# The same tiles at other addresses: small SBUF tiles first, a filler, and every large tile at a multiple of 2048 bytes

## The reference

```python
x = first_block(...)   # modulated rmsnorm, w_in, causal pooling + chunked state-space mixer, w_out, then PEER
x = second_block(...)  # rmsnorm, w_in (7 x 1024 columns), RG-LRU + gated conv, w_out, then PEER, rmsnorm
def peer(h, ...):      # product-key retrieval of single-neuron experts, 8 heads, top 16 of 16384 experts
    s1, s2 = q1 @ sub_keys1.T, q2 @ sub_keys2.T      # 128 + 128 keys per head
    idx, gates = top16 of (top16(s1) + top16(s2)), softmax
    act = gelu(h . expert_down[idx]);  out = sum(gates * act * expert_up[idx])
```

## Time and profile before

| | |
|---|---|
| median of 3 runs | 2038.16 us (2026.67, 2038.16, 2045.39) |
| profiled execution, its own time | 2028.78 us |
| its span, first to last instruction | 2027.0 us |
| TensorE matmul busy | 1974.7 us, 97% of the span |
| VectorE / ScalarE busy | 1506.5 us (74%) / 1013.7 us (50%) |
| granted TensorE clock, mean | 0.99 |
| DMA | 440.82 MB, mean 217 GB/s |

### The profile page before, as it was taken

One profiled execution on the slowest core, in us unless ns is written; L12 is line 12 of the kernel. 1 busy time (PEld: TensorE's weight loads), 2 busy tenths in 40 slices (PEclk: granted clock), 3 DMA queues, 4 the chain that ended last, 5 costly groups with the idle time before them and its releaser, 6 DMA issues.

```text
span 2027.0 us, 37752 instructions
## 1 busy us (share of the span) xinstructions
PE 1974.7 (97%) x14131; PEld 1830.3 (90%) x14131; DVE 1506.5 (74%) x2593; ACT 1013.7 (50%) x1358; POOL 0.2 (0%) x4
## 2 busy tenths in 40 slices
PE   7999899999999999999999999999999999999998
PEld 6988899999999888888799999999999998888886
DVE  5766769987886666666679665699878866666666
ACT  3651444455555444454546554444555554444444
POOL 0000000000000000000000000000000000000000
PEclk8999999999999999999999999999999999999999
DMA  7645767776556778777655654788766567777776
GB/s 269 207 169 206 270 194 249 243 240 213 182 182 212 244 238 243 240 241 244 209 167 155 189 158 145 229 248 240 242 209 183 181 214 242 240 242 240 237 246 197
DMA packets 135020, 440.82 MB, mean 217 GB/s; under 512 B 14976, under 2 KB 15232, under 8 KB 131200
## 3 DMA queue, kind: packets, MB, share of 16 engines
q1 hardware_dynamic: 117056, 406.84, 64.4%
q10 hardware_dynamic: 17856, 32.51, 4.4%
HBM read 403.64 MB, written 35.65 MB: 217 GB/s over the span
## 4 chain that ended last, share of the span: by engine, by line
PE 89%; DVE 6%; DMA 3%; ACT 2%; issue 1%; SPq 0%; DVEq 0%; ACTq 0%
PE ps L553 27%; PE ps L554 27%; PE ps L555 27%; PE ps L847 3%; DVE ring_lo L371 2%; DMA ring<-in_w_in 2%; PE ps L590 1%; ACT ring_hi L365 1%; PE ps L696 1%; DVE arena L1840 1%; PE ps L823 1%; PE ps L546 0%; DMA ring<-in_down 0%; DVE arena L1351 0%; DMA xT<-kept_x_spill 0%
## 5 line engine op out<-in xcount | busy, mean ns | idle before, releaser
L371 DVE TENSOR_TENSOR ring_lo<-ring,ring_hi 128x1024 fp32r<-128x1024 f32 x632 | 772.4, 1223 | 298.4 <-ACT ring_hi L365 290.4
L365 ACT ACTIVATE ring_hi<-ring 128x1024 fp32r<-128x1024 f32 x632 | 668.1, 1057 | 623.5 <-PE ps L555 470.3
L553 PE MATMUL ps<-h_hi,ring_lo 128*128 128x256 f32 x2816 | 799.0, 284 | 20.4 <-DVE ring_lo L371 9.4
L554 PE MATMUL ps<-h_lo,ring_hi 128*128 128x256 f32 x2816 | 786.8, 279 | 0.0
L555 PE MATMUL ps<-h_hi,ring_hi 128*128 128x256 f32 x2816 | 786.7, 279 | 0.0
L553 PEld LDWEIGHTS ps<-h_hi,ring_lo 128*128 128x128 f32 x2816 | 535.5, 190 | 24.9 <-issue 20.8
L554 PEld LDWEIGHTS ps<-h_lo,ring_hi 128*128 128x128 f32 x2816 | 535.2, 190 | 0.4 <-issue 0.2
L555 PEld LDWEIGHTS ps<-h_hi,ring_hi 128*128 128x128 f32 x2816 | 532.7, 189 | 0.0
L555 PE MATMUL ps<-ring_hi,w_hi 128*128 128x512 f32 x1024 | 398.4, 389 | 0.0
L554 PE MATMUL ps<-ring_lo,w_hi 128*128 128x512 f32 x1024 | 398.4, 389 | 0.0
L553 PE MATMUL ps<-ring_hi,w_lo 128*128 128x512 f32 x1024 | 398.4, 389 | 0.0
(11 more groups left out here) (284 smaller groups left out, 1287.7 us busy)
## 6 DMA issues: line engine op xcount, KB each, us to landing
ring<-in_down SPq DMA_DIRECT2D x256, 512.0 KB, 4.3
ring<-in_up SPq DMA_DIRECT2D x256, 512.0 KB, 4.0
ring<-in_w_in SPq DMA_DIRECT2D x80, 512.0 KB, 3.7
kept_z<-wf ACTq DMA_DIRECT2D x124, 256.0 KB, 3.3
xT<-kept_z SPq DMA_DIRECT2D x124, 256.0 KB, 4.3
arena<-in_w_ada SPq DMA_DIRECT2D x24, 1024.0 KB, 10.1
ring<-in_wq SPq DMA_DIRECT2D x32, 512.0 KB, 4.3
ring<-in_w_out_ssd SPq DMA_DIRECT2D x8, 512.0 KB, 4.2
```

The costliest lines, as they stand in the source:

```text
L365: nc.scalar.activation(ring_hi[:, part_slot(m), :], ring[:, slot(m), :], ACT.Copy).then_inc(S("high"), 1)
L371: ns.tensor_tensor(ring_lo[:, part_slot(n), :], ring[:, slot(n), :], ring_hi[:, part_slot(n), :].bitcast(fp32), ALU.subtract)\
L553: mm(psum, s_lo, m_hi, start=start, stop=False)
L554: mm(psum, s_hi, m_lo, start=False, stop=False)
```

## The change

The thirteen small tiles (`prm`, `iota16`, `ident16`, `mask16`, `mod`, `cact`, `epsc`, `lru_s`, `gain`, `sums_of`, `eps2`, `roots`, and a new one of 400 bytes that nobody reads or writes, `gap`) are allocated before all others. They end at byte 4096 of each partition with the 1152 bytes taken before and the rounding. All other tiles follow in the order they had. No instruction is added, removed or moved on any engine, and none has another shape: only the addresses in them differ.

```diff
+        prm = sb("prm", [P, NCOL])
+        iota16 = sb("iota16", [P, HD, 2], fp16)
+        ident16 = sb("ident16", [P, P], bf16)
+        mask16 = sb("mask16", [P, P], bf16)
+        mod = sb("mod", [P, 48])
+        cact = sb("cact", [P, 8])
+        epsc = sb("epsc", [P, 1])
+        lru_s = sb("lru_s", [P, 8, 8])
+        gain = sb("gain", [P, KC])
+        sums_of = sb("sums_of", [P, KC, 2])
+        eps2 = sb("eps2", [P, 2])
+        roots = sb("roots", [P, TT, 2])
+        gap = sb("gap", [P, 100])
         xT = sb("xT", [P, KC, T])
 
         h_hi = sb("h_hi", [P, KC, T], fp32r)
         h_lo = sb("h_lo", [P, KC, T], fp32r)
-        prm = sb("prm", [P, NCOL])
         cst = sb("cst", [P, NCONST])
         ring = sb("ring", [P, RING, BLK])
...
         sel16 = sb("sel16", [P, T // 4, 2, 2, 4, 2], fp16)
-        iota16 = sb("iota16", [P, HD, 2], fp16)
...
-        lru_s = sb("lru_s", [P, 8, 8])
         xs_lo = sb("xs_lo", [P, KC, T], fp32r)
-        gain = sb("gain", [P, KC])
...
-        roots = sb("roots", [P, TT, 2])
```

More of the change, by code:

```diff
@@ L104, in decoder_kernel @@
         sel16 = sb("sel16", [P, T // 4, 2, 2, 4, 2], fp16)
-        iota16 = sb("iota16", [P, HD, 2], fp16)
[L106 to L110, removed]
-        lru_s = sb("lru_s", [P, 8, 8])
         xs_lo = sb("xs_lo", [P, KC, T], fp32r)
-        gain = sb("gain", [P, KC])
-        sums_of = sb("sums_of", [P, KC, 2])
-        eps2 = sb("eps2", [P, 2])
-        roots = sb("roots", [P, TT, 2])
         ps_all = ctx.enter_context(nc.psum_tensor("ps", [P, 8, 512], fp32))
```

## The result

The change made the kernel slower: 2061.9 us (median of 4 runs, 2061.05 to 2063.38) against 2034.76 us (4 runs, 2026.67 to 2045.39), a ratio of 1.0134 with a 95% interval of 1.0098 to 1.017. The profiled execution took 2061.34 us with a span of 2059.5 us, 32.5 us more than before. The forecast was 25 us less; what came was most of the rival in which the two streams of TensorE collide.

A forecast was written before the change was run, and what follows sets the result against it. PE, busy 97% of the span, was taken to bound the kernel through the pace of the split products. 2028.8 - 20.6 - 3.9 = 2004.3 us, with 4.7 added for the median, gave 2009 us; range 1978 to 2068 us.

The forecast's parts named there:

- What bounds the kernel: PE is busy 97% of the span; only a changed pace of the split products can move the time by much.
- Up products: 3072 multiplies of 512 columns, moving tile from rest 64 to 0: 6.7 ns less each, 20.6 us; bounds 0 and 41.
- Residual products: 576 multiplies with `w_hi`, `w_lo` or `xs_lo` moving go from 120.0 to 113.3 ns: 3.9 us less.
- The `h_hi`/`h_lo` products: 8448 multiplies, moving tile already at rest 0 by 128: taken as 0; bounds 13 us less, 43 us more.
- The slower rival: Moving reads collide with next weights' loading at equal rests; `h_hi` products go to 120.0 ns, 43 us more, 2076 us; chance 0.22.
- No change: Rival: the paces 120.0 and 226.7 come from something other than the address; about 2034 us; chance 0.34.
- Faster still: Rival: up products reach 213.3 ns and the slow pace of `h_hi` products ends; 1971 us; chance 0.10.
- All other work: VectorE and ScalarE durations differ below 1% by address, 2 us at most; DMA taken as 0.
- The spread: The runs' spread of 19 us fits the two paces of the `h_hi` products and was expected to stay.

The follow-up runs named there:

- those at 64 and 192: The changed kernel with `h_hi` and `h_lo` moved to a rest of 64 or of 192 bytes: 2044.87 us (ratio 1.0064) and 2031.44 us (ratio 0.9988).
- the last kernel: The changed kernel with `w_hi` and `w_lo` moved by 64 bytes, so the up products get a difference of 192: 2081.01 us, ratio 1.0257.
- the one at 112: The changed kernel with `h_hi` and `h_lo` at a rest of 112 by 256, other large tiles at 0: 2019.75 us, ratio 0.9947.
- the mixed pairs: Stand-alone streams with tiles of one pair at different offsets: `m_lo` alone at 64 took 120.1 ns, `m_hi` 118.9, `s_hi` 122.1, `s_lo` 117.8.

## Why the prediction was wrong

**What bounds the kernel** was right: only the pace of the split products could move the time, and it did.

**The step that failed is "Up products", and "Residual products" with it.** The 120.0 ns of `w_hi`/`xs_lo` against the 113.3 ns of `h_hi` was read as the rest of the *moving* tile by 128. It was a difference of 0 against one of 192 to the *stationary* tile. The prediction said itself that the rows couldn't part the two. Forecast were -20.6 and -3.9 us; the up products moved by 0.0 us (696.16 both times, 884 records both times), the residual products by nothing that counts (120.0 ns still, their sum 1.9 us longer). Their difference was 0 before and after. The bounds of the first, 0 and -41 us, held by their upper end. Both terms sat on one inference; with it fell 24.5 us. The measured 2061.9 us lies inside the stated range of 1978 to 2068 us, but that is no merit of the forecast: the range was 90 us wide, and it reached that far for a change in which only part of the products pays, where nearly all did.

**"The `h_hi`/`h_lo` products" at 0** was mis-sized: 38.0 us in their records, 34.1 us between starts. Its upper bound was 43 us, for all products at 120.0 ns, and the unbroken distances did grow by 40.1 us. The rest of the miss is what the bound left out: the distances across pauses fell by 5.9 us. PE's idle time fell with them, and the waits above show the supply further ahead of a slower PE. What I had argued, "a pace that differs on equal addresses is set by something else", was half right: what stands ahead of a row does choose, but among paces that the addresses allow. At difference 0 there is one, 120.0; at 192 there are two.

**The slower rival** had the right pair of addresses and the right products, down to its mark, "if 300 to 400 us counts about 836, the collision is right": 835. That the loss comes from the moving read meeting the load of the next weights is not shown by this: the runs show that the pace goes by the two addresses, not what meets what. The rival's time, 2076 us, was 14 us too high. 9 us of this are the 34.1 for 43, and 1.6 us are other work that took less on balance. The last 4 us are in the 4.7 us added for a median above the profiled execution: after the change the median is only 0.6 us above it (2061.34 to 2061.9). The one argument against it, "the plain products meet the same rests and run at 216", said nothing: plain fp32 has 215.8 ns a record at all four pairs of offsets tried. A record of it takes nearly twice the time of an fp32r multiply for the same 256 columns, and I had used it as evidence on the faster one. I had also taken one record for a multiply; there are two, so a plain multiply of 256 columns takes 431.7 ns, and its 216 ns was no measure for 512 columns.

**"No change"** rested on the fact that plain fp32, VectorE and ScalarE show no address. That stays true where it was measured: plain fp32 at four pairs of offsets, VectorE and ScalarE only before and after the change. fp16 multiplies were not tried at other offsets. The rule that stood beside it, from the Trainium skill (SBUF — State Buffer, the box on SBUF "cachelines"), has a cost only for crossing to a new line of 16 bytes. By it the change does nothing; the ratio of 1.0134 decides against it as a full account. 112 is a multiple of 16, but so are 0 and 128, at 120.0 and 118.7 ns.

**"Faster still"** fell: no offset took 512 columns below 226.6 ns. The Trainium skill (TensorE: Matmul & The Clock Gate, Back-to-back issue gap) has 216 ns for a warm multiply of 512 columns by itself. No run here reached it in fp32r.

**All other work at 0** held: VectorE 1224 for 1223 ns, ScalarE 1057 for 1057, and the cover held in the up half. The term had "2 us at most"; PE's other multiplies took 2.6 us less.

**The spread.** That the runs of before spread over 19 us because of the two paces is likely, but not shown. For it: the three kernels whose `h` products have a difference of 0 spread over 1.3 to 2.3 us in four runs each, those at 64 and 192 over 8 and 11 us in 6 and 10 runs. Against it: the kernel before spread over 19 us in four runs and over only 4 us in the seven beside the last kernel, and the one at 112, which ends at one pace, over 7.6 us in 8. No two executions of one kernel were traced, so their shares of slow rows weren't compared.

**What stays open.** What in the memory repeats every 256 bytes; why 112 is good and 108 and 116 are not; what ahead of a row chooses between 113.3 and 117.8 ns; and the mixed pairs. Nor is it known whether the stationary tile that counts is the multiply's own or that of the next, whose weights load meanwhile: in all unmixed cases both lie alike.

## What to carry to other kernels

Where fp32r multiplies of 256 columns run back to back, look at the difference of the addresses of moving and stationary tile by 256, not at the alignment of either: the same start for everything cost 120.0 ns a multiply there for 113.3, and was the best choice for 512 columns. Only a few offsets are good, and four bytes beside one of them the gain was gone. If a row of the trace supports a cause in one operand, ask what the other operand did in the same rows; where they changed together, a forecast needs both readings at equal chance. And equal instructions on equal addresses may run at two paces in one execution; the count of records in two like stretches shows it.

## What the runs showed of the hardware

- An fp32r multiply of 256 columns had paces from 113.3 to 123.4 ns at the same clock and with nothing to wait for, by the difference of two addresses modulo 256 bytes (120.0 at 0, 118.7 at 128); plain fp32 (215.8 ns a record, two records a multiply) and fp32r multiplies of 128 and 192 columns (111.3 to 111.9 ns) had one pace at all differences tried.
- With 512 columns a difference of 0 was the best: 226.6 ns stand-alone and 226.7 in the kernels, 229 to 237 ns at the others tried.
- Equal instructions on equal addresses settled within a few multiplies at one of two paces (113.3 or 117.8 ns) and kept it; 6 of 17 starts were fast with difference 64, 17 of 23 with 192. The same lead-in gave the same distances to within 1 ns, twelve times of twelve.
- At 112 bytes every one of 26 starts ended at 113.3 ns, after 6 to 11 distances of up to 122 ns; 108 and 116 bytes cost 5 and 7 ns more over a segment.
